# Eleven homes for expert pieces instead of ten, a unit of block 2 in a slot of its own, and post-norms cut by column halves

## The chip, the cores and the metric

The kernel runs on one core of a Trainium2 chip. The metric is the device time of one execution in microseconds (us). The median of three runs of the kernel before is 1320.74 us (1318.24, 1320.74 and 1326.63).

## The reference, cut to what matters

Two transformer blocks on 256 tokens of width 1024, in float32. Block 1 is a mixer (attention and a convolution), cross-attention to a memory, and a mixture of 32 experts; then a final norm. Block 2 has two mixers side by side (HGRN2 and sparse attention), whose outputs are gated, merged and projected, then an MLP and a gated per-layer embedding.

```
# block 1, the experts: every expert runs on all tokens, gates are zero for tokens not routed to it
out = (jax.nn.silu(t @ wg) * (t @ wu)) @ wd
y = y + ge[:, None] * out
x = x + y;  x = rmsnorm(x, final_g)

# block 2, the three places with a norm behind a product ("post-norm")
x = x + rms_norm(merged @ w_out, norm_post_mix)
x = x + rms_norm(relu(h @ w_up)**2 @ w_down, norm_post_mlp)
x = x + rms_norm((p @ w_ple) * sigmoid(x @ w_ple_gate), norm_ple)
```

Here rms_norm(y, w) is y / sqrt(mean(y*y) + eps) * w over the 1024 columns. The router picks two experts of one group for each token. The weights of the 32 experts are 3 x 32 x 512 x 1024 values, 201 MB of the 333 MB that the kernel reads.

## The kernel before, in words

**Memory.** `ring` has 6 slots of 16 KB in each of the 128 partitions; `arena` has 12 pages of 8 KB; `spare` has one more 16 KB. Pages 12 to 23 are the second half of the ring under another name, and `parts_of_page` names all of it a third time for rounded copies.

**Queue of loads.** SyncE (SP) issues nearly all loads, in one written order; each waits on a semaphore for its place to be free, and a load that waits holds all behind it. Weights other than the experts' come as "units" of 2 MB (1024 x 512 values). `unit_at` gives each a slot; `load` waits for the last unit in that slot. The 17 units of block 2's first projections (`NAMES_2`: hq0, hq1, hf0, hf1, hi0, ...) are loaded as two halves of 1 MB each (`by_halves`), with a semaphore for each half.

**Experts.** The experts go four at a time (a "quad", 8 quads), each in 12 pieces of 2 MB: 4 gate, 4 up, 4 down. Piece m goes to place m mod 10 of `expert_places`: five slots' and pages' worth in the arena and ring and the spare. Ten early pieces are issued during cross-attention and routing as their places fall free (`early_piece`). After that `load_pieces` issues piece m when piece m - 10 was used. TensorE (PE) waits for each piece in `piece`, multiplies it with the gathered tokens (L939 gate and up, L967 down), and ScalarE and VectorE apply the activation. `gain_final` (the gain of the final norm) is loaded by GpSimd (POOL) into page 11 after the routing product `route1`, and used by VectorE at L1818 at the start of block 2.

**Block 2, projections.** A unit's product is made of three rounded products: ScalarE (ACT) rounds half a unit (`split_high`, L2214), VectorE (DVE) makes the rest in place (`split_rest`, L1424), PE takes both (`part_pairs`, L579 or L596). The rounded half has one buffer for each half, so rounding half h of the next unit waits for PE's use of half h of the one before. `first_projection` (L1063) does hq0, `split_feature_major` (L579) hq1, hf0 and hf1. Slots 0 and 1 alternate, so hf0 is loaded into slot 0 when hq0's product is done.

**Block 2, post-norms.** `add_normed` (L2080 to L2083) waits for both column halves of a token half t (128 tokens): square sum over 1024 columns (L1376), ScalarE's root (L2175), reciprocal (L1350), product with the gain (L1378), addition to x (L2083). It is called after `out2`, after `down` and, at the end, after `ple_gate`. After `out2`, `normalize_half` (L1369 to L1371) follows. After `down`, DVE first makes four rests of `ple_gate` (L1431), then both norms, then `half_rest` (L1440). PE in that time does the product `ple` (L1305, 16 matmuls), 18 idle products, the transposes of x (`x_half(0)`), 40 idle products (L512, they keep PE busy with numbers that nobody reads), and then the last pair `ple_gate` (L656, 96 matmuls with one set of transposes among them). The result goes out in two loads of 512 KB (L2686).

## Time and profile before

| | |
|---|---|
| profiled execution, its time | 1317.96 us |
| its span | 1316.2 us |
| median of three runs | 1320.74 us |
| PE busy | 1141.5 us (87%) |
| PEld (weight loads) busy | 845.1 us (64%) |
| DVE busy | 661.3 us (50%) |
| ACT busy | 439.3 us (33%) |
| POOL busy | 9.1 us |
| HBM read | 330.43 MB, 252 GB/s over the span |
| PE clock granted, mean | 0.945 |

Shares are means over stages that differ: in the experts the loads run without a break, elsewhere PE hardly rests. So the table says little of what one change is worth; the rows of the stage do. In timelines, one line merges instructions of the same kind; the times are start and length in us from the span's start, and brackets at the end give the idle time of the engine just before, and what ended it.

### The profile page before, as it was taken

The page shows a single profiled execution, that of the slowest core. Times are in us where ns is not written, and L with a number is a line of the kernel's source. Part 1 is how long each engine was busy: PE and PEld are TensorE (multiplying, and loading weights), DVE is VectorE, ACT ScalarE, POOL GpSimd, SP SyncE. Part 2 cuts the span into 40 slices and gives each one's busy share as a digit, 9 for nine tenths or more (in the row PEclk, how much of TensorE's full clock was granted, in tenths as well). Part 3 has the DMA queues.
Part 4 walks back from the last instruction along what each step waited for, and adds up shares of the span by engine and source line. Part 5 has one row for each costly group of instructions (what it writes and reads, how often), then busy time and mean ns, then how long its engine had stood idle before and what let it go on. Part 6 is the DMA issues. An engine that isn't in the chain of part 4 may idle for free.

```text
span 1316.2 us, 17044 instructions
## 1 busy us (share of the span) xinstructions
PE 1141.5 (87%) x7280; PEld 845.1 (64%) x7280; DVE 661.3 (50%) x1044; ACT 439.3 (33%) x624; POOL 9.1 (1%) x19
## 2 busy tenths in 40 slices
PE   7999999986666666657669999999999999999997
PEld 6987888732121132212128988878888889998875
DVE  5998745601000100101015799884877856554473
ACT  4237424110000000000016556443477524553342
POOL 0000000000000000000000000000000000000000
PEclk9999999998788877989889999999999999999999
DMA  9543483599999999999995534333553154445430
GB/s 363 206 162 146 173 334 133 218 426 427 428 427 428 428 426 428 427 428 428 427 425 196 165 128 156 129 128 128 193 192 128 42 214 168 171 176 191 161 120 32
DMA packets 27437, 332.61 MB, mean 253 GB/s; under 512 B 3184, under 2 KB 3456, under 8 KB 4960
## 3 DMA queue, kind: packets, MB, share of 16 engines
q1 hardware_dynamic: 26336, 328.47, 63.1%
q0 software_dynamic: 1024, 3.02, 0.8%
q8 instruction: 59, 0.97, 0.3%
q14 instruction: 18, 0.15, 0.0%
HBM read 330.43 MB, written 1.05 MB: 252 GB/s over the span
## 4 chain that ended last, share of the span: by engine, by line
PE 59%; DMA 28%; DVE 8%; ACT 3%; issue 2%; DVEq 0%; ACTq 0%
PE ps L579 12%; DMA ring<-in_w_down 10%; DMA ring<-in_w_gate 10%; PE ps L656 9%; PE ps L596 9%; PE ps L1289 7%; DMA ring<-in_w_up 6%; PE ps L939 3%; PE ps L761 2%; PE ps L688 2%; DVE parts L1424 2%; PE ps L512 1%; PE ps L743 1%; DMA ring<-in_units 1%; PE ps L967 1%
## 5 line engine op out<-in xcount | busy, mean ns | idle before, releaser
L1424 DVE TENSOR_TENSOR parts<-ring,parts 128x2048 fp32r<-128x2048 f32 x70 | 159.9, 2290 | 114.3 <-ACT parts L2214 113.9
L2214 ACT CAST parts<-ring 128x2048 fp32r<-128x2048 f32 x70 | 133.1, 1904 | 156.1 <-PE ps L579 62.5
L596 PE MATMUL ps<-parts 128*128 128x512 f32 x768 | 180.2, 392 | 1.5 <-DVE parts L1424 1.5
L579 PE MATMUL ps<-parts 128*128 128x256 f32 x1344 | 164.9, 285 | 2.2 <-DVE parts L1424 2.2
L579 PEld LDWEIGHTS ps<-parts 128*128 128x128 f32 x1344 | 163.4, 194 | 2.6 <-issue 2.4
L596 PEld LDWEIGHTS ps<-parts 128*128 128x128 f32 x768 | 142.6, 188 | 32.8 <-issue 3.7
L1742 DVE TENSOR_TENSOR arena<-arena,ps 128x512 f32<-128x512 f32 x32 | 21.9, 687 | 233.1 <-PE ps L977 232.2
L656 PE MATMUL ps<-parts 128*128 128x512 f32 x576 | 136.3, 395 | 0.5 <-DVE parts L1591 0.4
L939 PE MATMUL ps<-ring,arena 128*32 128x512 f32 x608 | 87.3, 706 | 47.5 <-DMA ring<-in_w_up 23.8
L656 PEld LDWEIGHTS ps<-parts 128*128 128x128 f32 x576 | 108.4, 190 | 23.4 <-issue 1.1
L939 PEld LDWEIGHTS ps<-ring,arena 128*32 128x32 f32 x608 | 18.5, 120 | 114.4 <-issue 41.2
L1289 PE MATMUL ps<-parts 128*128 128x512 f32 x384 | 87.3, 389 | 0.0
L1289 PEld LDWEIGHTS ps<-parts 128*128 128x128 f32 x384 | 72.0, 188 | 14.9
L939 PE MATMUL ps<-arena 128*32 128x512 f32 x320 | 50.1, 757 | 32.3 <-DMA arena<-in_w_gate 18.7
L1749 DVE TENSOR_TENSOR arena<-arena,ps 128x512 f32<-128x512 f32 x8 | 5.5, 687 | 125.4 <-PE ps L939 125.4
L967 PE MATMUL ps<-ring,arena 128*32 128x512 f32 x304 | 42.7, 690 | 23.1 <-DMA ring<-in_w_down 21.3
L2348 ACT COPY arena<-ps 128x512 f32<-128x512 f32 x8 | 4.7, 586 | 163.4 <-PE ps L948 163.4
L939 PEld LDWEIGHTS ps<-arena 128*32 128x32 f32 x320 | 10.0, 123 | 69.1 <-issue 29.7
L1431 DVE TENSOR_TENSOR parts<-ring,parts 128x2048 fp32r<-128x2048 f32 x22 | 49.7, 2287 | 9.0 <-ACT parts L2220 8.9
L1483 DVE SCALAR_TENSOR_TENSOR arena<-arena,cols 128x256 f32<-128x256 f32 x120 | 48.5, 476 | 0.0
L2346 ACT ACTIVATE arena<-ps 128x512 f32<-128x512 f32 x8 | 4.8, 597 | 129.0 <-PE ps L939 129.0
L2220 ACT CAST parts<-ring 128x2048 fp32r<-128x2048 f32 x22 | 41.1, 1906 | 10.5 <-PE ps L656 4.7
(357 smaller groups left out, 1445.9 us busy)
## 6 DMA issues: line engine op xcount, KB each, us to landing
ring<-in_units SPq DMA_DIRECT2D x34, 2048.0 KB, 8.2
ring<-in_units SPq DMA_DIRECT2D x39, 1024.0 KB, 5.2
ring<-in_w_gate SPq DMA_DIRECT2D x19, 2048.0 KB, 46.2
ring<-in_w_up SPq DMA_DIRECT2D x19, 2048.0 KB, 45.3
ring<-in_w_down SPq DMA_DIRECT2D x19, 2048.0 KB, 45.5
arena<-in_w_gate SPq DMA_DIRECT2D x11, 2048.0 KB, 45.8
arena<-in_w_down SPq DMA_DIRECT2D x10, 2048.0 KB, 45.1
arena<-in_w_up SPq DMA_DIRECT2D x9, 2048.0 KB, 45.4
```

What stands on the lines that cost most here:

```text
L579: mm = nc.tensor.matmul(banks[f][:, half * T:half * T + T], w[:, k, at:at + P], v[:, 4 * h + k, :], start=h + half + k + n == 0, stop=h + ...
L596: mm = nc.tensor.matmul(banks[t], v[:, 4 * h + k, t * P:t * P + P], w[:, k, :], start=h + k + n == 0, stop=h == 1 and k == 3 and n == 2)
L656: mm = nc.tensor.matmul(bank, a, b[:, j, :], start=k + n == 0, stop=k == KT - 1 and n == 2)
L688: mm = nc.tensor.matmul(banks[u, c][:, to:to + P], w[u][:, k, at:at + P], rhs[:, k, t * P:t * P + P], start=k == 0, stop=k == KT - 1)
L939: mm = nc.tensor.matmul(ps[e * CAP:e * CAP + CAP, bank, :], picked[:, 2 * u + k, e * CAP:e * CAP + CAP], w[:, e, k, :], start=u + k == 0, ...
L967: mm = nc.tensor.matmul(ps[e * CAP:e * CAP + CAP, down_banks[c], :], hiddenT[:, 2 * u + k, e * CAP:e * CAP + CAP], w[:, e, k, :], start=u ...
L1289: mm = nc.tensor.matmul(tiles[t], v[:, 4 * h + k, t * P:t * P + P], w[:, k, :], start=k4 + h + k + n == 0, stop=k4 == 3 and h == 1 and k = ...
L1424: step(V.tensor_tensor(rest_half(name, h), split_half(name, h), w_high[stage][h].bitcast(F32), ALU.subtract), f"{stage}_rest_ready", wait= ...
L1431: step(V.tensor_tensor(rest_half(name, h), split_half(name, h), pair_high[stage][2 * c + h].bitcast(F32), ALU.subtract), "pair_rest_ready" ...
L1483: ins = V.scalar_tensor_tensor(out=conv[:, cb, :], in0=z[:, cb, w:w + T], scalar=tap(w, cb), in1=conv[:, cb, :], op0=ALU.mult, op1=ALU.add)
L2214: step(S.copy(w_high[stage][h], split_half(name, h)), f"{stage}_high_ready", wait=False)
L2220: step(S.copy(pair_high[stage][2 * c + h], split_half(name, h)), "pair_high_ready", wait=False)
```

## The change

- `expert_places` has 11 places. The new one is "apart": pages 11 and 2 of the arena, 8 KB each, which do not lie side by side. A piece in it is loaded by two DMAs of 1 MB (`load_half`), and PE waits for 32 counts. The order of the places changes too; the early pieces are eleven, issued at the same events as the ten before, the halves of piece 7 among them: page 11 behind piece 8, page 2 (which held `xT`) after `route1`.
- `gain_final` moves from page 11 to page 10, which is an expert place. Its load now waits until the last piece in pages 9 and 10 (piece 89 of 0 to 95) was used. The router's scratch moves from page 11 to page 4.
- `FIRST_SLOTS`: hq0 and hq1 swap slots, and hf0 gets slot 3, whose last piece is 91. It is loaded as one DMA of 2 MB behind hq1. From hf1 on, slots alternate as before.
- Post-norms: the square sum is made by column halves (`half_sums`), each as soon as that half is there, and src is multiplied by the gain by halves. What follows the last half is: square sum over 512 columns, the sum of both with eps, product with the gain over 512 columns (during the root), reciprocal, and one instruction that multiplies by the reciprocal and adds x. At the end that instruction is cut in two halves, and the result goes out in four stores of 256 KB.
- After `down`: DVE makes the first half sums and two of the rests of `ple_gate` ahead of the norms, the other two rests behind `half_rest` of the first token half. PE transposes x's first token half between the two column halves of `ple`; both blocks of idle products are gone.

```diff
+FIRST_SLOTS = [1, 0, 3]
-        logits = grid(page(11, 0, 72), TT)
-        scratch_route = page(11, 128, 896)
+        logits = grid(page(4, 1024, 72), TT)
+        scratch_route = page(4, 1152, 896)
-        gain_final, gain_mix = page(11, 1024, 1024), page(12, 0, 1024)
+        gain_final, gain_mix = page(10, 0, 1024), page(12, 0, 1024)
-                slot = m % 2 if m < 17 else LATE_SLOTS[m - 17] if m < 25 else (2, 0, 1, 6)[(m - 25) % 4]
+                slot = FIRST_SLOTS[m] if m < 3 else m % 2 if m < 17 else LATE_SLOTS[m - 17] if m < 25 else (2, 0, 1, 6)[(m - 25) % 4]
-        expert_places = [("pages", 9), ("slot", 5), ("slot", 3), ("slot", 4), ("pages", 5), ("pages", 7),
-                         ("slot", 0), ("slot", 1), ("slot", 2), ("spare", 0)]
+        expert_places = [("spare", 0), ("pages", 9), ("slot", 5), ("slot", 3), ("slot", 4), ("pages", 5), ("pages", 7),
+                         ("apart", (11, 2)), ("slot", 1), ("slot", 0), ("slot", 2)]
         def by_halves(name):
-            return split_at.get(name, ("", 0))[0] == "proj"
+            return split_at.get(name, ("", 0))[0] == "proj" and unit_at[name][1] < 2
...
                             mm = nc.tensor.matmul(bank, pT[:, k, t * P:t * P + P], w[:, k, c * 512:c * 512 + 512], start=k == 0, stop=k == 1)
                         close_bank(mm, f"ple{c}{t}")
+                    if c == 0:
+                        x_half(0)
                 unit_last_fill["ple"] = "ple11"
-                idle_products(18)
-                x_half(0)
-                idle_products(40)
                 half_turned("pleT", 0)
...
-                def add_normed(src, k, t, gain, done="dve_step"):
-                    scaled_norm(src, normed[:, t, :], k, t, gain, normed[:, t, :])
-                    step(V.tensor_tensor(x[:, t, :], x[:, t, :], normed[:, t, :], ALU.add), done)
+                def half_sums(src, k, t, c, gain):
+                    cut = slice(c * 512, c * 512 + 512)
+                    step(V.tensor_tensor_reduce(normed[:, t, cut], src[:, t, cut], src[:, t, cut], 1.0 / D, 0.0, ALU.mult, ALU.add,
+                                                stat(k + 2 * t + c, 1)))
+                    if c == 0:
+                        step(V.tensor_tensor(src[:, t, cut], src[:, t, cut], gain[:, cut], ALU.mult), wait=False)
+                def add_normed(src, k, t, gain, done="dve_step", cuts=1):
+                    v = stat(k + 2 * t, 1)
+                    step(V.tensor_scalar(v, v, stat(k + 2 * t + 1, 1), EPS, ALU.add, ALU.add), "variance_ready", wait=False)
+                    step(V.tensor_tensor(src[:, t, 512:1024], src[:, t, 512:1024], gain[:, 512:1024], ALU.mult), wait=False)
+                    inverse_root(v)
+                    for c in range(cuts):
+                        cut = slice(c * D // cuts, (c + 1) * D // cuts)
+                        step(V.scalar_tensor_tensor(out=x[:, t, cut], in0=src[:, t, cut], scalar=v, in1=x[:, t, cut], op0=ALU.mult, op1=ALU.add),
+                             done, wait=cuts == 1)
...
-                for c in range(2):
-                    for h in range(2):
-                        pair_rest("ple_gate", c, h)
                 for t in range(TT):
-                    drained_by(dve, f"down0{t}", f"down1{t}")
+                    drained_by(dve, f"down0{t}")
+                    half_sums(mlp_out, 8, t, 0, gain_mlp)
+                for h in range(2):
+                    pair_rest("ple_gate", 0, h)
+                for t in range(TT):
+                    drained_by(dve, f"down1{t}")
+                    half_sums(mlp_out, 8, t, 1, gain_mlp)
                     add_normed(mlp_out, 8, t, gain_mlp, "x_ready")
-                for t in range(TT):
-                    half_rest("pleT", last_high, last_rest, t)
+                half_rest("pleT", last_high, last_rest, 0)
+                for h in range(2):
+                    pair_rest("ple_gate", 1, h)
+                half_rest("pleT", last_high, last_rest, 1)
...
-                filled_by(pool, "route1")
+                pool.wait_ge(sem("moe_piece_used"), SIDE * (last_piece_in(("pages", 9)) + 1))
                 pool.dma_start(gain_final, d["final_g"].partition_broadcast(P)).then_inc(sem("final_gain_landed"), 16)
...
+                def load_half(m, h):
+                    quad, u = m // PIECES, m % PIECES
+                    src = by_piece[u // 4][:, 4 * quad + u % 4:4 * quad + u % 4 + 1, h * PAGE:h * PAGE + PAGE]
+                    sp.dma_start(expert_halves("moe", m)[h].unsqueeze(1), src).then_inc(expert_landed("moe", m)[0], 16)
...
-                for m, free in ((1, "out11"), (9, "out11"), (2, "mem_q01"), (6, "mem_q11"), (4, "crossO3"), (7, "mem_o01"), (5, "mem_o11"), (8, "mem_o11")):
+                for m, free in ((2, "out11"), (0, "out11"), (3, "mem_q01"), (9, "mem_q11"), (5, "crossO3"), (8, "mem_o01")):
                     filled_by(sp, free)
                     early_piece(m)
+                load_half(7, 0)
+                filled_by(sp, "mem_o11")
+                for m in (6, 10):
+                    early_piece(m)
+                filled_by(sp, "route1")
+                load_half(7, 1)
-                for n in range(n_early, n_early + 2):
+                for n in range(n_early, n_early + 3):
                     sp.wait_ge(sem("moe_piece_used"), SIDE * (last_piece_in(("slot", units[n][2])) + 1))
                     load(n)
```

## Rows read from the trace of the kernel before

**Rows 1.** The page: GB/s moved in 40 equal slices of 32.9 us.

```profile
GB/s 363 206 162 146 173 334 133 218 426 427 428 427 428 428 426 428 427 428 428 427 425 196 165 128 156 129 128 128 193 192 128 42 214 168 171 176 191 161 120 32
```

**Rows 2.** Windows at the experts' start: length, busy of five engines, clock, DMA share, GB/s.

```profile
255.00:260.00 5.00, 4.34 (x40) 3.38 (x44) 3.18 (x12) 0.00 (x0) 0.00 (x0) 1.00 0.38 156
260.00:265.00 5.00, 5.00 (x54) 1.44 (x47) 1.42 (x5) 0.00 (x0) 0.00 (x0) 1.00 0.64 190
```

**Rows 3.** Timeline of the SP queue: the first load after the ten early ones.

```profile
261.01 0.33 SPq L2625 DMA_DIRECT2D arena<-in_w_down  x1
```

**Rows 4.** The page's DMA issues: count, KB each, median us from issue to landing.

```profile
ring<-in_units SPq DMA_DIRECT2D x34, 2048.0 KB, 8.2
ring<-in_units SPq DMA_DIRECT2D x39, 1024.0 KB, 5.2
out<-arena SPq DMA_DIRECT2D x2, 512.0 KB, 2.6
arena<-in_final_g POOLq DMA_DIRECT2D x1, 512.0 KB, 9.2
```

**Rows 5.** Windows while loads of 1 MB run: conv units, and hf0's halves.

```profile
10.00:15.00 5.00, 4.88 (x32) 4.12 (x31) 2.47 (x5) 4.12 (x8) 0.00 (x0) 1.00 1.02 429
712.00:713.00 1.00, 1.00 (x11) 1.00 (x10) 0.00 (x0) 0.00 (x0) 0.18 (x1) 1.00 1.00 394
```

**Rows 6.** Timeline around hf0: PE on hq1, SP's loads, ACT's rounding, PE on hf0.

```profile
704.94 11.68 PE L579 MATMUL ps<-parts 128*128 128x256 f32 x96
705.13 21.54 SPq L2609 DMA_DIRECT2D ring<-in_units  x5
714.47 1.91 ACT L2214 CAST parts<-ring 128x2048 fp32r<-128x2048 f32 x1 [7.75 <-DMA ring<-in_units]
718.84 7.47 PE L579 MATMUL ps<-parts 128*128 128x256 f32 x48 [2.23 <-DVE parts L1424]
```

**Rows 7.** The clock behind two idle stretches of PE: two windows, one timeline line.

```profile
721.00:722.00 1.00, 1.00 (x6) 1.00 (x6) 0.00 (x0) 1.00 (x1) 0.00 (x0) 0.50 0.14 57
...
881.72 2.05 PE L1105 MATMUL ps<-arena 128*128 128x128 f32 x16 [1.91 <-DVE arena L1925]
...
880.00:885.00 5.00, 2.91 (x20) 2.63 (x21) 4.97 (x4) 2.82 (x3) 0.00 (x0) 1.00 0.64 210
```

**Rows 8.** Timeline behind out2, second token half: the norm's start, PE's next transposes.

```profile
1085.38 1.23 DVE L1376 CUSTOM_DVE_ANT_0 arena<-arena 128x1024 f32<-128x1024 f32 x1 [2.73 <-ACT arena L2230]
...
1092.55 1.09 PE L617 MATMUL ps<-consts,arena 128*128 128x128 f32 x8 [0.80 <-DVE arena L1371]
```

**Rows 9.** Timeline between down and ple_gate: DVE, PE and ACT.

```profile
1263.46 0.68 DVE L2123 COPY arena<-ps 128x512 f32<-128x512 f32 x1
1264.06 4.48 DVE L1431 TENSOR_TENSOR parts<-ring,parts 128x2048 fp32r<-128x2048 f32 x2
...
1269.94 7.03 PE L1305 MATMUL ps<-ring,arena 128*128 128x512 f32 x16
...
1271.22 0.59 ACT L2230 ACTIVATE arena<-ps 128x512 f32<-128x512 f32 x1
...
1282.90 1.29 DVE L1440 TENSOR_TENSOR parts<-ps,parts 128x512 fp32r<-128x512 f32 x2
1284.28 5.73 PE L656 MATMUL ps<-parts 128*128 128x512 f32 x24
```

**Rows 10.** Timeline of the end: the last products, the last norm's first and last instruction.

```profile
1290.64 16.57 PE L656 MATMUL ps<-parts 128*128 128x512 f32 x72
...
1308.71 1.22 DVE L1376 CUSTOM_DVE_ANT_0 arena<-arena 128x1024 f32<-128x1024 f32 x1
...
1311.92 1.22 DVE L2083 TENSOR_TENSOR arena<-arena 128x1024 f32<-128x1024 f32 x1
```

**Rows 11.** Groups by line and shape on DVE: count, busy us, mean ns, idle before.

```profile
L1378 DVE SCALAR_TENSOR_TENSOR arena<-arena,small,ring 128x1024 f32<-128x1024 f32 x6 | 7.7, 1285 | 0.2
L1376 DVE CUSTOM_DVE_ANT_0 arena<-arena 128x1024 f32<-128x1024 f32 x6 | 7.3, 1224 | 7.4 <-ACT arena L2230 7.3
L2137 DVE TENSOR_TENSOR arena<-arena 128x512 f32<-128x512 f32 x4 | 2.8, 691 | 9.0 <-ACT arena L2230 9.0
```

More of the change, by code:

```diff
@@ L397, in slot_view, with expert_halves @@
             return flat.rearrange("p (k n) -> p k n", k=k)
+        def expert_halves(tag, m):
+            if lies_apart(tag, m):
+                return [page(n) for n in expert_places[m % places_of[tag]][1]]
+            flat = expert_flat(tag, m)
+            return [flat[:, 0:PAGE], flat[:, PAGE:SLOT]]
         def expert_flat(tag, m):
@@ L404, in expert_flat, with lies_apart @@
             return arena[:, at * PAGE:at * PAGE + SLOT] if kind == "pages" else ring[:, at * SLOT:at * SLOT + SLOT]
+        def lies_apart(tag, m):
+            return expert_places[m % places_of[tag]][0] == "apart"
         def expert_view(tag, m):
-            return expert_flat(tag, m).rearrange("p (e k n) -> p e k n", e=SIDE, n=512)
+            halves = [h.rearrange("p (e k n) -> p e k n", e=SIDE // 2, n=512) for h in expert_halves(tag, m)]
+            return lambda e, k: halves[e // 2][:, e % 2, k, :]
         def expert_landed(tag, m):
@@ L927, in piece @@
                         if tag == "moe":
-                            pe.wait_ge(landed, before + 16 * ((PIECES * n + u) // n_places + 1))
+                            each = 32 if lies_apart(tag, PIECES * n + u) else 16
+                            pe.wait_ge(landed, before + each * ((PIECES * n + u) // n_places + 1))
                             return expert_view(tag, PIECES * n + u)
@@ L939, in product @@
                                     mm = nc.tensor.matmul(ps[e * CAP:e * CAP + CAP, bank, :], picked[:, 2 * u + k, e * CAP:e * CAP + CAP],
-                                                          w[:, e, k, :], start=u + k == 0, stop=u == 3 and k == 1)
+                                                          w(e, k), start=u + k == 0, stop=u == 3 and k == 1)
                                     if k == 1:
```

46 lines of the change are left out of this document (30 added, 16 removed).

## The prediction

> **What bounds the kernel now.** I read the page first, then the chain of waits, and then the timeline and the windows of each stage that the edits touch. The page's slices [rows 1] show one stage whose bound is plain: from slice 9 to slice 21 the loads run at 425 to 428 GB/s without a gap. These are the experts; PE waits there for pieces, and only bytes or bandwidth can shorten the stage. One piece is 2048 KB, 2.097 MB, so at 427 GB/s it takes 4.91 us. Outside that stage the loads move 42 to 363 GB/s, and PE is the engine that hardly rests: in the timeline its only wait of over 2 us in block 2 is the one of 2.23 us ahead of hf0 [rows 6]. At the end of each post-norm the bound is VectorE, because PE cannot start the next product before x is there [rows 8, 9], and behind the last product nothing but the norm and the store is left [rows 10]. The change touches all of these places, so I price five terms.
>
> **Term A, the eleventh place.** The stream of later pieces starts when the first piece was used, with a load issued at 261.01 [rows 3]. That event is PE's and does not move. Before it the transfers rest: the window 255 to 260 moved 156 GB/s x 5 us = 0.78 MB, 1.8 us of full rate, so the early pieces had ended at about 256.8; the next window moved 190 x 5 = 0.95 MB, 2.2 us, so data flowed again from about 262.8 [rows 2]. The gap is 6.0 us. One piece more fits into it (4.91 us), all the more since the final gain's 512 KB [rows 4], 0.52 MB or 1.2 us, leaves this place. The early loads would then end at 256.8 + 4.91 - 1.23 = 260.5, ahead of 262.8. So the saturated stretch carries 85 pieces instead of 86: -4.91. The gain's load now waits for piece 89 and so falls into the saturated stretch, ahead of the last pieces: +1.23. The two DMAs of the split piece: of pieces 7, 18, ..., 95, eight are in the stretch. The nearest rows are loads of 1 MB back to back at 429 GB/s and halves of hf0, beside small loads, at 394 [rows 5]; 2.097 MB at 394 is 5.32, +0.41 a piece, 3.3 for eight. A faster rate than 427 is nowhere to be seen, so the bounds are 0 and +3.3; I take 0, since the 429 was measured with the queue full, as it is here, and the 394 beside POOL's small loads. SP has nothing else to do between the issues: each waits behind a use of a piece that is ten or eleven pieces back. **A = -3.7**, bounds -3.7 and -0.4.
>
> A rule speaks against this edit, and its sentences can be left out. The Trainium skill, "DMA: Bandwidth & Descriptors", section Bandwidth, gives 341 GB/s for a transfer of 1 MB against 425 for 16 MB, a figure for single transfers. By it a split piece would take 6.15 instead of 4.93 us, an estimate of +9.8 for eight, and the sum below would be -4.8 instead of -14.6. The trace disagrees where loads of that size are queued (429).
>
> **Term B, hf0 in slot 3.** hf0's load was issued at 705.13, when hq0's product was done; ACT waited 7.75 us for it and rounded at 714.47, and PE, done with hq1 at 704.94 + 11.68 = 716.62, began hf0 at 718.84 [rows 6]: 2.23 us lost. Behind the idle time the clock stood at 0.50 [rows 7], the 1.2 GHz level, and 48 matmuls took 7.47 us, where the 96 ahead took 11.68, 5.84 for 48: 1.63 more. In the new order hf0's load needs pieces up to 91 used, four pieces (20 us) ahead of the last landing, so it is queued directly behind hq1 and lands some 5 us after it, long before 705. What is late next is ACT's rounding, which waits for the buffer: PE has used hq1's first half at 704.94 + 5.84 = 710.8, rounding takes 1.91 and the rest 2.29 on DVE (the same shape as the L1431 pair, 4.48 for two [rows 9]): ready at 715.0, ahead of 716.62. The loads queued behind: hf1 needs hq0 done, as hf0 did; hi0 comes one unit earlier than it did. The work of DVE and ACT there hangs on PE's fills, so it shifts along. The final gain's wait on DVE (L1818, after 705) is for a load some 30 us old. **B = -3.9** (2.23 + 1.63), bounds -2.2 (the clock falls all the same, at another place) and -3.9. I take -3.7, since PE hardly rests but for a few tenths at the factor's products.
>
> **Term C, norm behind out2.** The chain from the last copy was 1224 + 1285 + 1224 (the addition, same shape as L1376) plus small ones; now it is 691 (half sum) + 691 (gain, with ACT's root under it) + 1285 (product and addition in one) [rows 11], the small ones alike less some 0.4 of root. 3.73 becomes 2.67; with the root hidden about -1.3. But PE waited for it only 0.80 us [rows 8], then PE's own first half is the bound. At t = 0 I allow a tenth more. **C = -0.9**, bounds 0 and -1.3.
>
> **Term D, between down and ple_gate.** New order on DVE, from the copy at 1263.46 + 0.68 = 1264.1 [rows 9]: two half sums with gain, 2 x (0.72 + 0.69) = 2.9, to 1267.0; two rests, 4.48, to 1271.5; ACT's copy of down1 is there at 1271.22 + 0.59 = 1271.8; half sum 0.72, small 0.19, gain 0.69, reciprocal 0.20, product and addition 1.32: x's first half at 1274.95. Second half the same way, 3.15: 1278.1. Then `half_rest` 1.29: 1279.4, where it ended at 1284.2 before. ACT in between: root, copy, root, two copies of ple, two roundings, done at 1278.3, so not late. PE: 16 matmuls of ple took 7.03, eight take 3.5: to 1273.4, then it waits 1.5 us for x, transposes 1.0, eight more: 1279.5. Both engines arrive together, and ple_gate starts at 1279.6 instead of 1284.28. The two rests moved behind are done at 1279.4 + 4.5 = 1283.9; PE wants them after 24 matmuls (5.73), at 1285.3. The idle products cost nothing by themselves, since PE would have waited; their cover was for the clock. A wait of 2.23 us was followed by the lower clock, one of 1.91 was not [rows 6, 7]. With 1.5 I take it as held. **D = -4.7**, bounds -3.1 (clock falls, +1.6 as in B) and -5.7 (nothing late but PE itself, 1270.0 + 7.0 + 1.0 + 0.6).
>
> **Term E, the end.** From L1376's start at 1308.71 to the end of L2083 at 1313.14 [rows 10], 4.43. New: 0.72 + 0.19 + 0.69 + 0.20 + two instructions of 0.69 = 3.2; -1.2. The last store has 256 KB instead of 512 (2.6 us to landing [rows 4]); its bytes take 0.6 instead of 1.2, if the rest is fixed: -0.4, bounds 0 and -0.6. **E = -1.6**, bounds -1.2 and -1.8.
>
> **Sum.** -3.7 - 3.7 - 0.9 - 4.7 - 1.6 = -14.6. Against the profiled execution's 1317.96 this is 1303.4; against the median 1320.74 it is 1306.1. The profiled execution lies 0.02% under the lowest of the three runs, and I take a level midway, 1319.5: **1305 us**.
>
> **Rivals.**
> 1. *The clock falls once in a new place* (in D's 1.5 us wait, or elsewhere after the shift): +1.6, 1306.5. For it, the drop behind 2.23 us of idle; against it, none behind 1.91.
> 2. *The eleventh place gives nothing*, since the split pieces run at 394: A = -0.4 instead of -3.7, 1308.3. Against it, 429 with a full queue.
> 3. *Slower than before: the start-up of the second half is not hidden.* 1 MB lands in 5.2 us, 2 MB in 8.2 [rows 4], so two halves one after the other cost 2 x 5.2 - 8.2 = 2.2 us more. Eight pieces: +17.6 in the saturated stretch, and 1305 becomes 1322.6, over the median. It decides from 14.6 / 8 = 1.8 us a piece. Against it: whole pieces run back to back at 427 GB/s, so their start-ups are hidden, and [rows 5]. In a milder form half of the 2.2 shows: +8.8, 1313.8. The Trainium skill's figure for 1 MB (the section named under A) would make it this form; the trace's 429 speaks against that too.
> 4. *The end of the MLP does not start earlier* (DVE's new order is late, PE waits in the middle of ple and gives the 4.7 back): 1309.7.
>
> **Chances.** The forecast (all terms near their size) 0.58; rival 1 0.14; rival 2 0.11; rival 3 in full 0.04 and in its milder form 0.05; rival 4 0.08. Range: the bounds of A to E together reach further than their joint chance, so I take from 1299 (D and E at their better bounds, the low run level) to 1312 (rivals 2 and 4 with part of each other), which leaves rival 3 outside. About 1% is what a measurement of this kernel can tell from no change; faster by that means under 1307.5. The forecast and rival 1 lie under it, but by 1 to 2.5 us only, less than the runs of before differ (8.4), so they give it four fifths of their 0.72: 0.58. Within 1%: the rest of these and rivals 2 and 4 and most of rival 3, 0.38. Slower by over 1%: 0.04, rival 3 with start-ups dearer than the 2.2 that [rows 4] give, and a clock that also falls.
>
> **What would show it.** A: SP's first load after the early ones still near 261, eleven issued ahead of it, last piece landed 3.7 us earlier, slices at 425 or more; with rival 3 the slices fall under 400. B: no wait of ACT for in_units and none of PE ahead of hf0, the clock at 1.00 behind it. C: PE's transposes without the 0.80. D: ple_gate's first matmul 4.7 us earlier relative to the end of down, clock 1.00 there. E: 3.2 us from the last half's square sum to the last addition. The forecast is wrong if the sum of A and B at the end of hf1 is under 5 us, or if ple_gate starts no earlier than down's end + 12 us.

## The result, and the profile after

The changed kernel ran in 1304.55 us in the median of four runs (1302.26 to 1306.5). The kernel before, on the same chip in the same job, took 1319.49 (1315.26 to 1326.63). The ratio is 0.9885 with a 95% interval of 0.9856 to 0.9914: 14.9 us less, where the working gave 14.6, and a median 0.5 us under the forecast. The profiled executions are 1302.26 and 1317.96, 15.70 us apart. I divide these 15.70 us at marks that both traces have (first expert product, first product of hq0, end of hf1, first product of block 2's up, of ple, of ple_gate, and the ends of PE and DVE):

| stretch | before | after | difference | forecast |
|---|---|---|---|---|
| start to the first expert product | 258.95 | 258.78 | -0.17 | 0 |
| first expert product to hq0 (A) | 433.53 | 430.20 | -3.33 | -3.7 |
| hq0 to the end of hf1 (B) | 51.39 | 47.46 | -3.93 | -3.7 |
| end of hf1 to up (C lies in it) | 357.85 | 356.74 | -1.11 | -0.9 |
| up to ple | 168.2 | 168.2 | 0 | 0 |
| ple to ple_gate (D) | 14.34 | 9.18 | -5.16 | -4.7 |
| ple_gate to PE's end | 22.93 | 22.91 | 0 | 0 |
| PE's end to DVE's end (E) | 5.93 | 4.54 | -1.39 | -1.2 |
| store and the time around it (E) | | | -0.6 | -0.4 |

That the first row is near nothing is chance. The changed kernel's trace is 1.0 us later at the router's first product (PE at L902, 244.90, for L883 at 243.88), and the trace of before loses up to 1.7 us between 249 and 253, where its clock falls and that of the changed kernel does not. Between hf1 and up both traces have one such fall, so the -1.11 there is not the clock's.

**The experts.** The page's row of slices of the changed kernel answers to [rows 1]:

```profile
GB/s 364 200 145 150 162 335 179 257 399 427 426 428 426 428 426 426 428 427 427 427 424 303 124 130 148 144 130 130 195 177 148 25 171 186 195 195 193 163 130 33
```

The saturated stretch stays at 424 to 428. In windows of the changed kernel, with the columns of [rows 2], more moves in the stretch that used to rest:

```profile
255.00:260.00 5.00, 4.51 (x40) 3.38 (x44) 3.24 (x13) 0.00 (x0) 0.00 (x0) 1.00 0.93 390
260.00:265.00 5.00, 5.00 (x52) 1.56 (x48) 1.29 (x4) 0.00 (x0) 0.00 (x0) 1.00 0.71 231
```

390 x 5 = 1.95 MB where 0.78 MB moved, and 1.16 where 0.95 did. The timeline of the changed kernel, SP and POOL (time, length, engine, line, operation, in brackets what it waited for), shows that the first later load is still issued at PE's first use, at 260.84 [rows 3], now for piece 11 in the place that piece 0 left (spare), and that the final gain's load, on POOL's own queue, is issued while the last six pieces, issued by SP before it, are still to be used (piece 90 at 658.45):

```profile
260.84 0.33 SPq L2671 DMA_DIRECT2D spare<-in_w_down  x1
...
655.88 0.54 POOL L2605 DMA_DIRECT2D arena<-in_final_g  x1 [651.85 <-PE ps L959]
```

Two waits of PE late in the experts date the gain and what is given back of it. First before, then after; in each the first line is the fourth down piece of quad 6 (piece 83), the second the last up piece (piece 91):

```profile
628.80 1.92 PE L967 MATMUL ps<-ring,arena 128*32 128x512 f32 x16 [1.58 <-DMA ring<-in_w_down]
...
667.98 2.83 PE L939 MATMUL ps<-ring,arena 128*32 128x512 f32 x16 [2.97 <-DMA ring<-in_w_up]
```

```profile
624.12 3.64 PE L987 MATMUL ps<-arena 128*32 128x512 f32 x16 [1.64 <-DMA arena<-in_w_down]
...
664.31 3.55 PE L959 MATMUL ps<-ring,arena 128*32 128x512 f32 x16 [3.94 <-DMA ring<-in_w_up]
```

Piece 83 is used 4.68 us earlier, piece 91 only 3.67: between them lies the gain's load (655.88), and the wait has grown from 2.97 to 3.94.

**hf0.** In the changed kernel's timeline PE runs through from hq0 to hf0 as one group of 144 matmuls, where [rows 6] had 96, a wait of 2.23 and 48 more. ACT's rounding now waits for a buffer that PE gives, no longer for the load, and the clock in the window behind stays at 1.00 against the 0.50 of [rows 7]:

```profile
701.44 17.44 PE L598 MATMUL ps<-parts 128*128 128x256 f32 x144
...
707.45 1.90 ACT L2255 CAST parts<-ring 128x2048 fp32r<-128x2048 f32 x1 [4.23 <-PE ps L598]
```

```profile
715.00:720.00 5.00, 5.00 (x45) 5.00 (x43) 3.08 (x6) 1.42 (x3) 0.00 (x0) 1.00 0.46 184
```

**Behind out2** PE's transposes of the second token half carry no wait, where [rows 8] had 0.80:

```profile
1084.06 1.04 PE L636 MATMUL ps<-consts,arena 128*128 128x128 f32 x8
```

**From down to ple_gate and the end**, the changed kernel's timeline, which answers to [rows 9, 10]:

```profile
1258.19 4.49 DVE L1450 TENSOR_TENSOR parts<-ring,parts 128x2048 fp32r<-128x2048 f32 x2
...
1261.39 3.59 PE L1329 MATMUL ps<-ring,arena 128*128 128x512 f32 x8
...
1263.23 0.69 DVE L2102 CUSTOM_DVE_ANT_0 arena<-arena 128x512 f32<-128x512 f32 x1 [0.56 <-ACT arena L2271]
...
1264.89 1.28 DVE L2115 SCALAR_TENSOR_TENSOR arena<-arena,small 128x1024 f32<-128x1024 f32 x1
...
1266.23 1.09 PE L636 MATMUL ps<-consts,arena 128*128 128x128 f32 x8 [1.24 <-DVE arena L2115]
...
1267.16 3.60 PE L1329 MATMUL ps<-ring,arena 128*128 128x512 f32 x8
...
1269.18 1.29 DVE L1459 TENSOR_TENSOR parts<-ps,parts 128x512 fp32r<-128x512 f32 x2
1270.57 5.71 PE L675 MATMUL ps<-parts 128*128 128x512 f32 x24
...
1294.95 0.69 DVE L2102 CUSTOM_DVE_ANT_0 arena<-arena 128x512 f32<-128x512 f32 x1
...
1296.61 1.41 DVE L2115 SCALAR_TENSOR_TENSOR arena<-arena,small 128x512 f32<-128x512 f32 x2
```

The clock stays at 1.00 there (time, length, and behind the five engines the clock, DMA share and GB/s):

```profile
1265.00:1270.00 5.00, 3.77 (x15) 2.27 (x16) 4.86 (x9) 2.64 (x6) 0.00 (x0) 1.00 0.00 0
```

PE waits 1.24 us for x between the two column halves of ple, then has eight matmuls left, and ple_gate starts 9.18 us after ple, not 14.34. Behind the last product DVE needs 4.54 us.

### The profile page after: what moved, and what is told of

The parts are those of the page before. It is cut to its first block, busy times and chain, and to the rows that moved or that the text cites. A ratio compares the mean times of both kernels' runs of the same rounds, so it can differ in the third digit from the quotient of the medians.

```text
span 1300.5 us, 16955 instructions
## 1 busy us (share of the span) xinstructions
PE 1127.3 (87%) x7222; PEld 836.5 (64%) x7222; DVE 662.6 (51%) x1064; ACT 439.3 (34%) x624; POOL 9.1 (1%) x19
## 4 chain that ended last, share of the span: by engine, by line
PE 57%; DMA 29%; DVE 8%; ACT 3%; issue 2%; SPq 0%; DVEq 0%; another core or an unknown queue 0%; ACTq 0%
PE ps L598 12%; DMA arena<-in_w_down 11%; DMA arena<-in_w_gate 11%; PE ps L675 9%; PE ps L615 9%; PE ps L1309 6%; DMA ring<-in_w_down 3%; PE ps L707 2%; PE ps L780 2%; DMA arena<-in_w_up 2%; PE ps L959 2%; DVE parts L1443 1%; PE ps L762 1%; PE ps L987 1%; DMA ring<-in_units 1%
## 5 line engine op out<-in xcount | busy, mean ns | idle before, releaser
L959 PE MATMUL ps<-ring,arena 128*32 128x512 f32 x528 | 76.2, 709 | 53.9 <-DMA ring<-in_w_up 28.7
L959 PE MATMUL ps<-arena 128*32 128x512 f32 x416 | 59.7, 707 | 30.7 <-DMA arena<-in_w_gate 17.7
L1309 PEld LDWEIGHTS ps<-parts 128*128 128x128 f32 x384 | 72.0, 188 | 14.9
L959 PEld LDWEIGHTS ps<-arena 128*32 128x32 f32 x416 | 13.2, 122 | 77.2 <-issue 35.9
L987 PE MATMUL ps<-ring,arena 128*32 128x512 f32 x288 | 38.4, 666 | 18.4 <-DMA ring<-in_w_down 16.1
```

Of the source, the lines that this page charges most:

```text
L959: mm = nc.tensor.matmul(ps[e * CAP:e * CAP + CAP, bank, :], picked[:, 2 * u + k, e * CAP:e * CAP + CAP], w(e, k), start=u + k == 0, stop=u ...
L987: mm = nc.tensor.matmul(ps[e * CAP:e * CAP + CAP, down_banks[c], :], hiddenT[:, 2 * u + k, e * CAP:e * CAP + CAP], w(e, k), start=u + k == ...
L1309: mm = nc.tensor.matmul(tiles[t], v[:, 4 * h + k, t * P:t * P + P], w[:, k, :], start=k4 + h + k + n == 0, stop=k4 == 3 and h == 1 and k = ...
```

## The experiments

Each experiment alters the changed kernel in one respect. Its median is compared with the kernel before, run in the same job, and its trace with that of the changed kernel, stretch by stretch. The stretches are the finer measure: in several traces the clock falls once more or once less between the end of hf1 and up, or ahead of the experts, at 1.7 us a time, and the medians carry that. The stretches have a spread of their own: from ple to ple_gate the seven traces with the changed kernel's work there (the changed kernel's, experiments 1 to 4, 9 and 10) take 8.68 to 9.18 us, the first of them 9.18. The last experiments repeat two of the kernels and the changed one, to see how far that goes.

### Experiment 1: hf0 back behind hq0 in one slot (B)

```diff
-FIRST_SLOTS = [1, 0, 3]
+FIRST_SLOTS = [0, 1, 0]
```

> The changed kernel with hf0 back in slot 0 behind hq0 (hq0 in slot 0, hq1 in slot 1, as before). Theory: all that term B gave was the wait for hf0's load and the low clock behind it. ACT should wait some 7.7 us for the load again, PE 2.2 us ahead of hf0, and hf0 to hf1 end 3.9 us later than in the changed kernel (736.5 there); if the clock falls too, hf0's 48 products take 7.5 us instead of 5.8. Time 1304.5 + 3.9 = 1308.4. Rival: the deeper loading also helps the units behind hf1 (hi0 comes a unit earlier); then the distance grows to 5 us or more by the end of the projections. Second rival: PE's wait returns but the clock does not fall, as the stage now lies at another time: +2.2, 1306.7.

Measured: 1309.15 us (1307.14 to 1310.28) against 1318.53, ratio 0.9916 (0.9893 to 0.9939). From the timeline of this kernel:

```profile
713.89 1.91 ACT L2255 CAST parts<-ring 128x2048 fp32r<-128x2048 f32 x1 [7.80 <-DMA ring<-in_units]
...
718.26 4.02 PE L598 MATMUL ps<-parts 128*128 128x256 f32 x23 [2.28 <-DVE parts L1443]
```

The waits of before are back (7.80 and 2.28, for 7.75 and 2.23 in [rows 6]), and so is the fall of the clock: hq0 to the end of hf1 takes 51.44 us, +3.98. The whole of B hangs on this one line: hf0's place, and with it that it comes in one load and that hq0 and hq1 are swapped, which were not taken apart. Nothing more is lost behind hf1 than one further fall of the clock (358.39 us to up, for 356.74), so the rival of a gain beyond hf1 is not borne out.

### Experiment 2: ten places (A)

```diff
-        gain_final, gain_mix = page(10, 0, 1024), page(12, 0, 1024)
+        gain_final, gain_mix = page(11, 1024, 1024), page(12, 0, 1024)
...
-        expert_places = [("spare", 0), ("pages", 9), ("slot", 5), ("slot", 3), ("slot", 4), ("pages", 5), ("pages", 7),
-                         ("apart", (11, 2)), ("slot", 1), ("slot", 0), ("slot", 2)]
+        expert_places = [("pages", 9), ("slot", 5), ("slot", 3), ("slot", 4), ("pages", 5), ("pages", 7),
+                         ("slot", 0), ("slot", 1), ("slot", 2), ("spare", 0)]
...
-                load_half(7, 0)
...
...
-                filled_by(sp, "route1")
-                load_half(7, 1)
```

The final gain's load, the router's scratch and the order of the early pieces are back too.

> The changed kernel with the ten places, the order of early pieces, the router's scratch and the final gain of the kernel before; terms B to E stay. Theory: the eleventh place is worth 4.91 us of loading less 1.23 us for the gain's load in the full stretch, so PE's first product of hq0 starts 3.7 us later than in the changed kernel, near 692.5, and the time is 1304.5 + 3.6 = 1308. Rival: the place is worth nothing by itself and the stage moved by where the clock fell around the router (it fell there in the kernel before and not in the changed one): then hq0's products start where they do in the changed kernel, within 0.5 us, once the start of the experts is subtracted.

Measured: 1308.99 us (1308.16 to 1309.61), ratio 0.9922 (0.9899 to 0.9944). In the timeline of this kernel, piece 91 and the first product of hq0:

```profile
667.53 3.64 PE L959 MATMUL ps<-ring,arena 128*32 128x512 f32 x16 [1.89 <-DMA ring<-in_w_up]
...
693.31 2.15 PE L1083 MATMUL ps<-parts 128*128 128x256 f32 x16
```

From the first expert product to piece 91 it is 667.53 - 258.37 = 409.16 us, for 409.03 before and 405.53 after: the eleventh place with all that it carries is worth 3.6 us. That hq0 starts 4.7 us later than in the changed kernel, relative to the first expert product, is 1.1 us of PE's own behind piece 91, where the clock was low for longer.

### Experiment 3: every piece by two DMAs (A's split, rival 3)

```diff
-                        loads[at] += 16
+                        loads[at] += 32
...
-                            each = 32 if lies_apart(tag, PIECES * n + u) else 16
+                            each = 32
...
-                    if tag == "moe" and lies_apart(tag, m):
+                    if tag == "moe":
```

The stream of later pieces then has 85 split pieces instead of 8.

> The changed kernel, but every expert piece, not one in eleven, is loaded by two DMAs of 1 MB (to neighbouring pages where the place is whole). 85 pieces in the full stretch are split instead of 8, so whatever a split costs is seen ten times over. Theory: with the queue full a split costs nothing: the time stays within 3 us of 1304.5 and the slices of the experts at 425 GB/s or more. Rival 2 (394 GB/s for transfers of 1 MB): 77 more pieces x 0.41 = +32 us. Rival 3 (start-up of the second half not hidden): 77 x 2.2 = +169 us; in its milder form, 1.1 each, +85 us.

Measured: 1312.95 us (1308.4 to 1313.64), ratio 0.9946 (0.9922 to 0.997). The page's slices and one of its DMA issues, and then two lines of the timeline:

```profile
GB/s 361 208 159 151 165 322 156 263 420 421 421 421 421 422 420 421 422 422 421 422 420 289 127 129 148 141 128 128 193 140 183 4 182 193 194 190 180 176 128 32
...
ring<-in_w_down SPq DMA_DIRECT2D x36, 1024.0 KB, 26.9
```

```profile
669.71 3.64 PE L959 MATMUL ps<-ring,arena 128*32 128x512 f32 x16 [4.34 <-DMA ring<-in_w_up]
...
695.60 2.15 PE L1083 MATMUL ps<-parts 128*128 128x256 f32 x16
```

Loads of 1 MB in a full queue run at 420 to 422 GB/s, for 426 to 428 in loads of 2 MB. Piece 91 comes 411.41 us after the first expert product, +5.9, and hq0 7.1 later. So a split costs 5.9 / 77 = 0.08 us, or 7.1 / 77 = 0.09 at most, since 1.2 of the 7.1 lie behind piece 91, where PE's clock stood at 0.50 for longer than in the changed kernel. Eight splits cost some 0.6 to 0.7. My expectation, that a split costs nothing (within 3 us, slices at 425 or more), failed by these figures, but neither 394 GB/s (+32 us), nor 2.2 us a piece (rival 3), nor half of it is anywhere near.

### Experiment 4: the final gain behind the last piece (A's other side)

```diff
-                pool.wait_ge(sem("moe_piece_used"), SIDE * (last_piece_in(("pages", 9)) + 1))
+                pool.wait_ge(sem("moe_piece_used"), SIDE * PIECES * QUADS)
```

> The changed kernel with one wait moved: the final gain's 512 KB are loaded when the last expert piece was used instead of piece 89. Theory: the load then no longer lies ahead of the last pieces, which land 1.2 us earlier. In the changed kernel PE had no wait ahead of the last piece, though, and spends 1.7 us in idle products there, so only a part shows: 0 to 0.4 us, 1304.3. DVE takes the gain at about 705 and the load takes 9 to 11 us from its issue near 686, so it is there by 697. Rival: the last pieces still set the end of the stage, and all of the 1.2 us shows: hq0's products start 1.2 us earlier. Rival on the other side: the load comes late for the multiplication of x (L1818's successor), which delays the factor's product in hf0: +1 us or more.

Measured: 1302.8 us (1301.41 to 1303.24), ratio 0.987 (0.9847 to 0.9892). In its timeline:

```profile
663.19 1.92 PE L959 MATMUL ps<-ring,arena 128*32 128x512 f32 x16 [1.57 <-DMA ring<-in_w_up]
...
687.54 2.15 PE L1083 MATMUL ps<-parts 128*128 128x256 f32 x16
```

The wait of 3.94 is 1.57 and hq0 starts 429.01 us after the first expert product, -1.19: all of the gain's 1.23 us, where I had expected no more than 0.4 to reach hq0: the first rival came true. The load costs its bytes in the stream, and the stream's end sets hq0.

### Experiment 5: post-norms whole (C, D and E)

```diff
                 def half_sums(src, k, t, c, gain):
+                    return
...
                 def add_normed(src, k, t, gain, done="dve_step", cuts=1):
-                    v = stat(k + 2 * t, 1)
...
+                    scaled_norm(src, normed[:, t, :], k, t, gain, normed[:, t, :])
                     for c in range(cuts):
                         cut = slice(c * D // cuts, (c + 1) * D // cuts)
-                        step(V.scalar_tensor_tensor(out=x[:, t, cut], in0=src[:, t, cut], scalar=v, in1=x[:, t, cut], op0=ALU.mult, op1=ALU.add),
+                        step(V.tensor_tensor(x[:, t, cut], x[:, t, cut], normed[:, t, cut], ALU.add), done, wait=cuts == 1)
```

> The changed kernel with its order of work kept, but the post-norms over whole rows: no half sums, one square sum of 1024, product with reciprocal and gain, then the addition (in two halves at the end, with the four stores kept). Theory: the halves shorten each norm by 1.0 to 1.3 us. Behind out2 PE gets back the 0.8 us of waiting (C undone, +0.9); between down and ple_gate DVE starts its rests 2.7 us earlier but has two longer norms in a row, 2 x 1.2 more behind the last copy: ple_gate starts 11.4 us behind ple's first product instead of 9.2; the end, from PE's last product to DVE's last addition, 5.6 us instead of 4.5. In all +4.3, 1308.8. Rival: the order of work did it all, and the norms by halves hide behind PE anyway: within 1.5 us of 1304.5, ple_gate 9.2 us behind ple's start.

Measured: 1311.01 us (1309.03 to 1312.39) against 1320.38, ratio 0.9933 (0.9912 to 0.9953). The timeline behind out2 and between ple's column halves, and a window behind the latter:

```profile
1086.33 1.09 PE L636 MATMUL ps<-consts,arena 128*128 128x128 f32 x8 [0.80 <-DVE arena L1390]
...
1269.82 1.56 PE L636 MATMUL ps<-consts,arena 128*128 128x128 f32 x8 [2.50 <-DVE arena L2113]
```

```profile
1270.00:1273.00 3.00, 3.00 (x11) 1.97 (x11) 2.63 (x5) 1.75 (x5) 0.00 (x0) 0.55 0.00 0
```

The wait of 0.80 of [rows 8] is back, and the stretch up to block 2's up is 1.15 us longer (C). From ple to ple_gate it is 11.93 us, +2.75 (PE waits 1.26 us more, and the clock falls to the lower level behind the wait); the end is 5.98, +1.44 (E). With 1.03 ahead of the experts, where the clock fell and in the changed kernel it did not, and 0.4 elsewhere, this makes the 6.77 us between the profiled executions, 1309.03 and 1302.26. That is 2.5 more than the 4.3 that I expected: 1.0 is the fall ahead of the experts, 0.55 lie in D with its fall, the rest is tenths in the other stretches.

### Experiment 6: all four rests ahead of the norms (D, DVE's order)

```diff
-                for h in range(2):
-                    pair_rest("ple_gate", 0, h)
+                for c in range(2):
+                    for h in range(2):
+                        pair_rest("ple_gate", c, h)
...
-                for h in range(2):
-                    pair_rest("ple_gate", 1, h)
```

> The changed kernel, but DVE makes all four rests of ple_gate ahead of the norms, as before the change (the two of column half 1 cost 4.5 us). Theory: x's first half comes some 4 us later, PE waits in the middle of ple for over 5 us instead of 1.24, and ple_gate starts 13.2 us behind ple's first product instead of 9.2: +4.0, and since no idle products fill the wait, the clock falls to the lower level behind it, as it did behind the 2.2 us ahead of hf0: +1.6 more, 1310.1. Rival: the clock holds, as the products of ple ahead of the wait count: +4.0, 1308.5. Other rival: the order of the rests does nothing, ACT's roundings set the time: under 1.5 us.

Measured: 1311.14 us (1310.24 to 1312.11), ratio 0.9933 (0.9912 to 0.9953). Its timeline, and a window behind PE's wait:

```profile
1259.56 8.89 DVE L1450 TENSOR_TENSOR parts<-ring,parts 128x2048 fp32r<-128x2048 f32 x4
...
1271.36 1.97 PE L636 MATMUL ps<-consts,arena 128*128 128x128 f32 x8 [5.00 <-DVE arena L2115]
...
1273.12 5.61 PE L1329 MATMUL ps<-ring,arena 128*128 128x512 f32 x8
```

```profile
1270.00:1275.00 5.00, 3.64 (x11) 2.61 (x12) 4.84 (x9) 2.17 (x6) 0.00 (x0) 0.53 0.00 0
```

DVE's two further rests (4.4 us) put 3.76 us on PE's wait, and the clock falls behind it: eight matmuls of ple take 5.61 instead of 3.60. From ple to ple_gate it is 15.40 us, +6.2, longer than before the change.

### Experiment 7: PE's order of before (D, PE's order)

```diff
-                    if c == 0:
-                        x_half(0)
...
+                idle_products(18)
+                x_half(0)
+                idle_products(40)
                 half_turned("pleT", 0)
...
-                    if c == 0:
-                        half_high("pleT", last_high, 0)
...
+                half_high("pleT", last_high, 0)
```

ACT's rounding of x's first half goes with it, back behind its copies of ple.

> The changed kernel, but PE's order between down and ple_gate as before: 16 products of ple, 18 idle products, transposes of x, 40 idle products; ACT's roundings of x behind all copies of ple. DVE's new order stays. Theory: idle products are no filler here any more but work on the path. PE: 7.0 + 2.1 + 1.0 + 4.5, so ple_gate starts 14.6 us behind ple's first product instead of 9.2: +5.4, 1309.9; the whole of term D is lost though DVE is as fast as in the changed kernel. Rival: DVE's order was all, PE's changes only moved the waiting: ple_gate 10 us behind ple's start or less, within 1.5 us of 1304.5.

Measured: 1309.42 us (1307.73 to 1310.21), ratio 0.9915 (0.9894 to 0.9936). Its timeline from ple to ple_gate:

```profile
1263.64 7.03 PE L1329 MATMUL ps<-ring,arena 128*128 128x512 f32 x16
...
1270.50 2.13 PE L531 MATMUL ps<-consts 128*128 128x256 bf16 x18
...
1272.47 1.04 PE L636 MATMUL ps<-consts,arena 128*128 128x128 f32 x8
1273.34 4.53 PE L531 MATMUL ps<-consts 128*128 128x256 bf16 x40
1277.63 2.54 PE L675 MATMUL ps<-parts 128*128 128x512 f32 x10
```

There is no wait of PE in these lines: the 58 idle products, written to fill a wait, stand on the path for 2.13 + 4.53 = 6.66 us. From ple to ple_gate it is 13.99 us, +4.8, though x is there as early as in the changed kernel. With experiments 5 and 6: any one part of D left out gives back between half and more than all of its 5.2 us. DVE's order and PE's order pay only together; with the norms whole about half of D is left, and that with a fall of the clock in it.

### Experiment 8: a version beyond the change

```diff
-                    for h in range(2):
+                    for h in range(2 - c):
...
+                        pair_split("ple_gate", 1, 1)
...
-                pool.wait_ge(sem("moe_piece_used"), SIDE * (last_piece_in(("pages", 9)) + 1))
+                pool.wait_ge(sem("moe_piece_used"), SIDE * PIECES * QUADS)
```

The gain's load is that of experiment 4, and ACT's last rounding for ple_gate moves from ahead of its copies of down to behind the rounding of x's first half.

> The changed kernel with the final gain's load behind the last expert piece (this took 1.2 us from the stage of the experts) and with ACT's last rounding of ple_gate (column half 1, row half 1) moved from ahead of the copies of down1 to behind the rounding of x's first half. In the changed kernel DVE waits 0.56 us for the copy of down1, which ACT makes behind that rounding. Theory: -1.2 for the gain and -0.5 for the copy, ple_gate 8.6 us behind ple's first product, 1302.8. Rival: the rounding then comes late for DVE's rest and PE's second column half: no gain at ple_gate's end. As the clock falls once, twice or three times in the middle of block 2 from run to run (1.7 us each), the time alone will not tell 0.5 us; the distances between events of a stage do.

Measured: 1305.22 us (1303.85 to 1306.4), ratio 0.9887 (0.9869 to 0.9905). From ple to ple_gate it is 8.54 us instead of 9.18, and hq0 starts 429.20 us after the first expert product instead of 430.20: 1.6 us of gains in the stretches that were meant, by this pair of traces. Of the 0.64 between ple and ple_gate only part is sure, as the changed kernel's work there took 8.68 us in another trace and 9.0 in the mean of seven. But ahead of the experts it lost 1.8 and between hf1 and up 2.8, with three falls of the clock between hf1 and up where the changed kernel's trace has one. The expected 1302.8 was missed.

### Experiments 9 to 11: the changed kernel and both versions again

Experiment 9 is the changed kernel, 10 the kernel of experiment 4, 11 that of experiment 8.

> The changed kernel itself, unaltered, beside the two versions with the late gain, on one chip and against the same runs of the kernel before. Theory: 15 us under the kernel before, as in the first measurement (0.9885). In its stages: first expert product to hq0 430.2 us, hq0 to the end of hf1 47.5, up1 to ple 168.2, ple to ple_gate 8.7 to 9.2, PE's end to DVE's end 4.5; the stretch between hf1 and up1 356.7 plus 1.7 for every further fall of the clock there. Rival: one of these distances was particular to the one profile, then it differs by over 0.5 us.

> As the run with the gain behind the last piece before, now beside the changed kernel. Theory: first expert product to hq0 1.2 us shorter than in the changed kernel (429.0 against 430.2), the other distances alike, the median 1.2 us lower. Rival: the median does not follow, since falls of the clock of 1.7 us each vary more from run to run than this gain; then the ratio to the kernel before agrees with the changed kernel's within its interval.

> As the run with the late gain and ACT's rounding moved, now beside the changed kernel. Theory: 1.2 us from the experts and 0.4 us between ple and ple_gate (8.5 against 8.9): the median 1.6 us lower than the changed kernel's, a ratio of 0.9873. Rival: no difference that the measurement can tell, as above.

| kernel | first job | again |
|---|---|---|
| changed | 1304.55, ratio 0.9885 (0.9856 to 0.9914) | 1305.29, 0.9893 (0.9872 to 0.9913) |
| gain behind the last piece | 1302.8, 0.987 (0.9847 to 0.9892) | 1305.7, 0.9899 (0.9878 to 0.992) |
| that and ACT's order | 1305.22, 0.9887 (0.9869 to 0.9905) | 1303.74, 0.9883 (0.9861 to 0.9905) |

The intervals overlap everywhere, so none of these is a kernel that beats the changed one; the late gain's median did not come out 1.2 us lower again, and that of experiment 11, 1.55 lower as expected, lies within its interval. The stretches do repeat: hq0 at 429.12 and 429.03 us after the first expert product for the late gain, 430.18 for the changed kernel; ple_gate 8.54 us after ple against 9.16 (9.07 in experiment 10). In experiment 11 the timeline has the shorter wait for x:

```profile
1268.10 1.09 PE L636 MATMUL ps<-consts,arena 128*128 128x128 f32 x8 [0.60 <-DVE arena L2115]
```

Two other stretches move by more than the 1.6 us. The first expert product comes at 258.78 us in the first trace of the changed kernel and at 262.09 in the second, where the granted clock was 0.57 in the mean from 248 to 256, and 1.00 there in the first. From hf1 to up it is 356.74 us in the first and 358.44 in the second, and 359.44 to 359.53 in the traces of experiments 4, 8, 10 and 11, for the same work. The last two differ, by 1.0 us, through a fall of the clock behind one wait of PE, which experiment 9 does not have (first line) and experiment 10 has (second):

```profile
877.56 2.05 PE L1125 MATMUL ps<-arena 128*128 128x128 f32 x16 [1.91 <-DVE arena L1944]
```

```profile
874.59 3.17 PE L1125 MATMUL ps<-arena 128*128 128x128 f32 x16 [1.91 <-DVE arena L1944]
```

All four traces with the late gain have this fall, and of the nine others only that of experiment 3. So it may be that the late gain brings it about and loses there what it wins ahead of hq0, or it may be chance; no run tells the two apart.

## Why the prediction was right, step by step

**What bounds the kernel** was read rightly: the five places are where the 15.70 us came from, and the two stretches between them that were to stay alike did. (Of the loads outside the experts it said 42 to 363 GB/s; the last slice of [rows 1] is 32. Nothing hangs on it.)

**A, -3.7 forecast, -3.33 measured.** The piece that fits into the gap gave -4.68 at piece 83, of which 0.17 is the earlier start, against -4.91. The gain's load in the saturated stretch took back 1.0 to 1.2 (the wait grown from 2.97 to 3.94, and -1.19 in experiment 4), against 1.23. The splits, taken at 0 between bounds of 0 and 3.3, cost some 0.6 to 0.7 by experiment 3. That is the one term of A off in size, and by itself more than the 0.4 that A came short; some 0.3 went the other way. The choice between the ends by the row of 429 GB/s, where loads of 1 MB were queued, and not by the 394 beside small loads, was sound. The Trainium skill, "DMA: Bandwidth & Descriptors", section Bandwidth, would have had 341 GB/s for loads of this size; the trace disagrees where the queue is full: 420 to 422.

**B, -3.7 forecast, -3.93 measured**, and experiment 1 brings both parts back, the wait and the clock. The 0.2 held back for the factor's products was not needed.

**C, -0.9 forecast, about -1.0.** The 0.80 is gone, and comes back with the whole norms. The rest of the stretch's -1.11 is as small as what differs between runs there.

**D, -4.7 forecast, -5.16 measured.** PE and DVE were to arrive together, with a wait of 1.5 us for x; it was 1.24, and the clock was held at 1.00. The prediction put x's first half at 1274.95 in the time of before, 5.01 us behind ple's start (1269.94); it was there at 1264.89 + 1.28 = 1266.17, 4.78 behind it (1261.39). The half rest, forecast to end at 1279.4, 9.46 behind that start, ended at 1269.18 + 1.29 = 1270.47, 9.08 behind. That and 0.1 us between the half rest and ple_gate are the 0.46 that D came out larger. A part of that is the trace: DVE waited 0.56 us for ACT's copy of down1 in this one and not at all in that of experiment 1, where D's stretch took 8.68. That a wait which is too long costs the clock as well was right: with the four rests ahead (experiment 6) it is 5.00 us and the clock falls. But the ground for holding the clock safe at 1.5 us, that a wait of 1.91 had not been followed by a fall, was one row. The same wait was followed by a fall in 5 of the 13 traces, so here there was some luck.

**E, -1.6 forecast.** -1.39 on DVE, where -1.2 was worked out, and -0.6 for the store and what lies around it, where -0.4 was; the four smaller stores were not tested by themselves. The page's issues of the changed kernel have stores of 256 KB at 2.0 us from issue to landing, for 2.6 at 512 KB [rows 4]:

```profile
out<-arena SPq DMA_DIRECT2D x4, 256.0 KB, 2.0
```

**The rivals.** The clock falling in D's new wait (1) did not happen. Elsewhere, which the rival also named, it falls a varying number of times: the second trace of the changed kernel has some 6.8 us of them, half ahead of the experts and half between hf1 and up, the first 1.7. The eleventh place giving nothing (2) falls with experiment 2, by 3.6 us. The start-up of the second halves (3), in full or by half, falls with experiment 3: 0.08 to 0.09 us a split instead of 2.2 or 1.1. The MLP's end not earlier (4) falls with the trace: 9.18 us.

**The level.** 1319.5 was taken between the profiled execution and the median; the kernel before gave 1319.49, 1318.53, 1320.38 and 1319.97 in the four jobs. That it was met to 0.01 us is luck: the fourth run, 1315.26, drew the median there. So is part of the 0.5 us between forecast and median, as single terms are off by up to 0.46 and the profiled executions are 15.70 us apart, not 14.6. The range of 1299 to 1312 was wider than needed on both sides. Its upper part was held for rivals 2 and 4.

## What to carry to other kernels

Where a stage is bound by bytes, look for where the queue rests just ahead of it: one buffer more whose load fitted in that rest took nearly a whole load off the stage here (4.5 of 4.91 us, before the gain's load), and two separate pages served nearly as well as one (0.08 us a piece), the queue being full. For the same reason a small load that has time should not be put ahead of the stage's last pieces: here it cost its bytes in full. And where two engines meet at one point, shortening one of them gives only as much as the other allows: price the norm, the order on VectorE and the order on TensorE as one term, and when the producer gets faster, look for filler products on the consumer, which turn from cover into work (6.66 us here).

## What was not expected of the hardware

- **What one more DMA costs.** 77 further splits cost 5.9 to 7.1 us: 0.08 to 0.09 us each with the queue full, though in the median a load of 1 MB takes 5.2 us from issue to landing and one of 2 MB 8.2 [rows 4].
- **Idle time and the clock.** Behind waits of PE of 2.23, 2.28 and 2.50 us and in one of 5.00 (before, experiments 1, 5, 6) the granted clock fell to 0.50, the 1.2 GHz level; behind the waits of 1.24 and 1.21 ahead of x's transposes (the two traces of the changed kernel) it stayed at 1.00. The length of a wait alone does not decide it. One wait of 1.90 to 1.92 us (L1125, above) was followed by a fall in five traces (experiments 3, 4, 8, 10, 11) and by none in the eight others. In the experts of the changed kernel PE waits 2.97 us twice in a row; behind the first its 16 matmuls take 1.92 us, behind the second 3.59:

```profile
638.86 1.92 PE L959 MATMUL ps<-ring,arena 128*32 128x512 f32 x16 [2.97 <-DMA ring<-in_w_gate]
643.75 3.59 PE L959 MATMUL ps<-ring,arena 128*32 128x512 f32 x16 [2.97 <-DMA ring<-in_w_gate]
```

- **The clock also falls where PE does not rest.** From hf1 to up the level falls one to three times a run (once in the trace of the changed kernel, twice in that of experiment 9, three times in experiments 4, 8, 10 and 11), mostly at a cost of 1.7 us each. One of these falls is in all 13 traces, at 957 to 973 us. In the changed kernel PE is busy without a wait in the 7 us ahead of it, at last with 64 small products, and in all five us of the window:

```profile
953.64 3.75 PE L1233 MATMUL ps<-ring,arena 64*128 64x15 f32 x64
```

```profile
957.00:962.00 5.00, 5.00 (x22) 3.98 (x21) 3.40 (x9) 4.97 (x14) 0.00 (x0) 0.66 0.07 30
```

  A mean of 0.66 over 5 us is the 1.7 us lost. In experiment 9 a second fall came earlier, behind two short waits of 0.67 and 1.04 us:

```profile
935.00:940.00 5.00, 3.29 (x28) 2.52 (x27) 4.83 (x9) 2.61 (x5) 0.00 (x0) 0.83 1.00 426
```

  The falls that come in one trace and not in the next are large enough to hide two gains of 0.5 and 1.1 us in the medians. What decides whether one comes was not settled.
